# Mixture-of-experts layer on one core: gate-up weights in rows of 32 KB, in places of 4 MB, and an add-back around half of the next gate-up

## The reference

```python
h = h + merged @ w_out[layer]
u = rms_norm(h, ffn_norm_gain[layer])
logits = u @ w_router + b_router
top_logit, top_idx = lax.top_k(logits, 4)          # of 32 experts
top_w = jax.nn.softmax(top_logit, axis=-1)
for e in range(32):                                # only the rows that chose e
    gu = xb @ w_gate_up[e] + b_gate_up[e]          # w_gate_up[e]: 1024 x 2048
    gate, up = jnp.split(gu, 2, axis=-1)
    gate, up = jnp.minimum(gate, 7.0), jnp.clip(up, -7.0, 7.0)
    act = (up + 1.0) * gate * jax.nn.sigmoid(1.702 * gate)
    y_rows = act @ w_down[e] + b_down[e]           # w_down[e]: 1024 x 1024
    h[rows] += y_rows * weight_of_e[rows]
```

## Time and profile before

| | us |
|---|---|
| median of 3 runs | 1256.24 |
| lowest and highest of them | 1252.46, 1256.24 |
| the profiled execution | 1254.52 |
| its span (first to last instruction) | 1252.7 |

### The profile page before, as it was taken

The page is one execution under the profiler, slowest core; times in us unless marked ns, Lnnn a source line. Parts: engine busy times, 40 slices in busy tenths (PEclk is TensorE's granted clock), DMA queues, the critical chain, the costliest instruction groups (busy, mean ns, idle before and its releaser), DMA issues.

```text
span 1252.7 us, 14150 instructions
## 1 busy us (share of the span) xinstructions
PE 1174.1 (94%) x5825; PEld 654.8 (52%) x5825; DVE 302.8 (24%) x551; ACT 133.3 (11%) x270; POOL 6.6 (1%) x14
## 2 busy tenths in 40 slices
PE   9999999999999999999898979898898889898998
PEld 7877888888633435434252534343443434353533
DVE  2154222311302321304030303122121303030322
ACT  2233311101200000101000000001010100000001
POOL 0000001000000000000000000000000000000000
PEclk9999999999999999999999999999999999999999
DMA  9722322336799999999999999999999999999996
GB/s 380 321 97 98 120 102 101 135 134 268 274 417 405 421 427 429 427 427 428 429 428 428 427 430 428 429 428 427 430 429 429 428 427 428 430 430 428 426 421 281
DMA packets 38002, 446.37 MB, mean 356 GB/s; under 512 B 4016, under 2 KB 5168, under 8 KB 6352
## 3 DMA queue, kind: packets, MB, share of 16 engines
q1 hardware_dynamic: 37344, 443.63, 84.8%
q10 hardware_dynamic: 624, 2.25, 0.5%
HBM read 444.81 MB, written 1.05 MB: 356 GB/s over the span
## 4 chain that ended last, share of the span: by engine, by line
PE 68%; DMA 28%; issue 1%; DVE 1%; SPq 0%; ACT 0%; DVEq 0%
DMA ring<-in_w_down 25%; PE ps L513 20%; PE ps L809 18%; PE ps L832 10%; PE ps L772 4%; PE ps L798 3%; DMA ring<-in_w_gate_up 3%; PE ps L863 2%; PE ps L881 2%; PE ps L818 1%; DVE arena L1440 1%; PE ps L853 1%; PE ps L827 0%; PE ps L572 0%; SPq L440 0%
## 5 line engine op out<-in xcount | busy, mean ns | idle before, releaser
L809 PE MATMUL ps<-ring,arena 128*64 128x512 f32 x1392 | 419.5, 613 | 38.7 <-DMA ring<-in_w_gate_up 30.7
L809 PEld LDWEIGHTS ps<-ring,arena 128*64 128x64 f32 x1392 | 137.0, 141 | 303.4 <-issue 303.4
L513 PE MATMUL ps<-arena,ring 128*128 128x256 f32 (+1 forms) x1184 | 268.1, 383 | 1.1 <-DVE arena L1321 1.1
L513 PEld LDWEIGHTS ps<-arena,ring 128*128 128x128 f32 x1184 | 221.0, 189 | 38.9 <-issue 6.6
L832 PE MATMUL ps<-ring,arena 128*64 128x512 f32 x672 | 197.9, 594 | 28.6 <-DMA arena<-in_w_down 18.5
L809 PE MATMUL ps<-arena 128*64 128x512 f32 x464 | 207.1, 599 | 0.0
L832 PEld LDWEIGHTS ps<-ring,arena 128*64 128x64 f32 x672 | 65.4, 137 | 144.9 <-issue 144.9
L1420 DVE COPY arena<-ps 128x1024 f32<-128x1024 f32 x16 | 19.6, 1225 | 421.9 <-PE ps L809 419.0
L832 PE MATMUL ps<-arena 128*64 128x512 f32 x224 | 99.0, 594 | 0.0
L1141 ACT ACTIVATE arena<-ps 128x1024 f32<-128x1024 f32 x16 | 16.4, 1024 | 560.3 <-PE ps L809 555.3
L1413 DVE TENSOR_TENSOR arena<-ps,arena 128x512 f32<-128x512 f32 x64 | 41.1, 684 | 143.2 <-PE ps L818 143.2
(11 more groups left out here) (210 smaller groups left out, 576.4 us busy)
## 6 DMA issues: line engine op xcount, KB each, us to landing
ring<-in_w_gate_up SPq DMA_DIRECT2D x95, 2048.0 KB, 26.9
ring<-in_w_down SPq DMA_DIRECT2D x47, 2048.0 KB, 24.7
arena<-in_w_gate_up SPq DMA_DIRECT2D x32, 2048.0 KB, 31.2
ring<-in_mix_w SPq DMA_DIRECT2D x37, 1024.0 KB, 5.5
arena<-in_w_down SPq DMA_DIRECT2D x16, 2048.0 KB, 26.1
ring<-in_w_down SPq DMA_DIRECT2D x2, 1024.0 KB, 30.6
arena<-in_consts ACTq DMA_DIRECT2D x1, 1424.0 KB, 12.0
arena<-in_xT SPq DMA_DIRECT2D x2, 544.0 KB, 4.4
```

The source lines that it names most:

```text
L513: last = mm(ps[:, PROJ + half, 0:rhs.shape[-1]], w[:, k, half * P:(half + 1) * P], rhs, start=(k == 0), stop=(k == KC - 1))
L809: last = mm(ps[half, bank + b], columns[:, j, half], w[x][:, at:at + 512], start=(j == 0), stop=(j == 7))
```

## The change

1. From pair 2 on (the third pair that the steady loop of loads serves) the gate-up weights come as four "quads" of 4 MB, each with four row blocks of one expert, 32 KB in each partition. There are four places of 4 MB: three quarters of the ring, and one stretch of `arena` (`last_quad`) that joins the two spare ones. Down units stay at 2 MB with 16 KB rows, two of them to a place.
2. SP waits for a place by halves of a gate-up or of a down step. PE's gate-up goes by halves too: `gate_up_quad(m, odd, h)` waits for two quads and does four row blocks.
3. `add_back` of pair m is split: groups 0 and 1 where it was, groups 2 and 3 behind the first half of the next pair's gate-up. The down bias is added in pair 2 instead of pair 1.
4. To let the stretches join, the constants are laid out in another order (the decay tables first, loaded by a third DMA of ACT), `r_u` and `con` move, and the row blocks of the hidden dimension are numbered by four instead of two, in all gate-up sources and in ACT's layout of the tokens (`u2tok`).
5. Ring slots shift by one (`slot_of`), the first gate-up units go to the doubles 0 to 5 and are issued one unit sooner, and the first unit of the second gate-up goes ahead of unit 7.
6. PE writes out pairs 2 and 3 as well; its loop starts at 4.

```diff
-    for name, n in (("ones", P), ("ident", P), ...
-                    ("tri", P), ("from_1", TOK), ("alibi", SCW), ("decay", RH * TOK), ("decay_meta", RH * TOK)):
+    for name, n in (("decay", RH * TOK), ("decay_meta", RH * TOK), ("ones", P), ("ident", P), ...
+                    ("tri", P), ("from_1", TOK), ("alibi", SCW)):
...
+        last_quad = arena[:, end_p - 2048:end_p + 6144]
+        spare = (last_quad[:, 0:4096], arena[:, end_rg - 4096:end_rg], last_quad[:, 4096:8192])
...
+        def slot_of(unit):
+            return (unit + SLOTS - 1) % SLOTS
+        homes = tuple((double(d), pair_landed[d]) for d in range(DOUBLES)) + ((spare[0], spare_landed[0]), (spare[2], spare_landed[2]))
+        def quad(m, n):
+            odd = m if isinstance(m, int) else 0
+            q = ((1 if odd % 2 else 3) + n) % 4
+            return last_quad if q == 3 else ring[:, 4 * q:4 * q + 4].rearrange("p a b -> p (a b)"), quad_landed[q]
+        def half_quad(odd, n):
+            return quad(odd, n // 2)[0][:, 4096 * (n % 2):4096 * (n % 2 + 1)]
...
+            def four_rows_source(lap, n):
+                h, x = divmod(n, 2)
+                return w_gate_up[bass.ds(2 * lap + x, 1), :, :].rearrange("o (h p j) n -> (o p) h (j n)", h=2, j=4)[:, h]
...
             def first_units():
                 for j in (0, 1, 2, 3, 7, 4, 5):
-                    if j < 3:
-                        sp.wait_ge(proj_done, 2 * (27 + 2 * j + 1))
-                    elif j in (3, 7):
+                    if j == 7:
                         sp.wait_ge(proj_read, AT[("wr", KC - 1)] + 1)
+                        dst, arrived, _ = place(0, 0)
+                        sp.dma_start(dst.rearrange("p (o n) -> p o n", o=2), both_experts_source(1, 0)).then_inc(arrived, 16)
                     else:
-                        sp.wait_ge(proj_done, 2 * (33 + 2 * (j - 4) + 1))
+                        sp.wait_ge(proj_done, 2 * (26 + 2 * j + 1))
...
+            def gate_up_quads(m, odd, lap):
                 for n in range(4):
+                    if n < 2:
+                        sp.wait_ge(gu_used, 8 * m + 6 + 2 * n)
+                    else:
+                        sp.wait_ge(dn_used, 4 * m - 6 + 2 * n)
+                    dst, arrived = quad(odd, n)
+                    sp.dma_start(dst, four_rows_source(lap, n)).then_inc(arrived, 16)
+            def down_halves(m, odd, lap):
+                for n in range(4):
+                    sp.wait_ge(gu_used, 8 * m + 10 + 2 * (n // 2))
+                    sp.dma_start(half_quad(odd, 8 + n), down_source(lap, n)).then_inc(down_landed[n], 16)
...
-                pair_units(m, 0, lap_1, lap_0)
-                pair_units(m + 1, 1, lap_2, lap_1)
-            last_gate_up_units(last_m)
-            last_down_units(last_m, 0, 14, 8, 1)
-            last_down_units(last_m + 1, 1, 15, 0, 2)
+                gate_up_quads(m, 0, lap_1)
+                down_halves(m, 0, lap_0)
+                gate_up_quads(m + 1, 1, lap_2)
+                down_halves(m + 1, 1, lap_1)
+            gate_up_quads(last_m, 0, 15)
+            last_down_units(last_m)
...
+            def gate_up_quad(m, odd, h):
+                w = []
+                for x in range(2):
+                    dst, arrived = quad(odd, 2 * h + x)
+                    pe.wait_ge(arrived, 16 * m - 16)
+                    w.append(dst)
+                for jj in range(4):
+                    j = 4 * h + jj
+                    for b in range(4):
+                        at = jj * 2048 + b * 512
+                        for x, half in enumerate(halves):
+                            last = mm(ps[half, GATE + b], xeT[:, j, half], w[x][:, at:at + 512], start=(j == 0), stop=(j == 7))
+                            if jj == 3 and b == 3:
+                                last.then_inc(gu_used, 2)
...
-                    for i in range(4):
-                        gate_up(i, lambda q: place(m, q, odd), xeT)
+                    for h in range(2):
+                        if h == 1 and odd is not None:
+                            add_back(m - 1, (2, 3))
+                        if odd is None:
+                            for i in (2 * h, 2 * h + 1):
+                                gate_up(i, lambda q: place(m, q), xeT)
+                        else:
+                            gate_up_quad(m, odd, h)
...
-                add_back(m, isinstance(m, int) and m == 1)
+                add_back(m, range(4) if isinstance(m, int) and m == 0 else (0, 1))
...
-            with pe.Fori(2, last_m, 2) as m:
+            pair(2, 0)
+            pair(3, 1)
+            with pe.Fori(4, last_m, 2) as m:
...
-                A(u2tok[:, t].rearrange("p (i j f) -> p i j f", i=4, j=2),
-                  ps[:, Y + 2 * t:Y + 2 * t + 2].rearrange("p b f -> p (b f)").rearrange("p (i f j) -> p i j f", i=4, j=2), ACT.Copy,
+                A(u2tok[:, t].rearrange("p (i j f) -> p i j f", i=2, j=4),
+                  ps[:, Y + 2 * t:Y + 2 * t + 2].rearrange("p b f -> p (b f)").rearrange("p (i f j) -> p i j f", i=2, j=4), ACT.Copy,
```

More of the change, by code:

```diff
@@ L79, in _const_layout @@
     at = 0
[L80 to L81 removed]
+    for name, n in (("decay", RH * TOK), ("decay_meta", RH * TOK), ("ones", P), ("ident", P), ("heads2", P), ("halves", 2), ("eps", 1), ("eps64", 1), ("slopes", 2 * HEADS), ("fold", EXPERTS),
+                    ("tri", P), ("from_1", TOK), ("alibi", SCW)):
         CONST_COLS[name] = (at, n)
@@ L87 @@
 N_CONST = _const_layout()
-N_CONST_EARLY = CONST_COLS["tri"][0]
+EARLY, LATE = CONST_COLS["ones"][0], CONST_COLS["tri"][0]
 PARAM_COLS = {}
@@ L221, in build @@
         tmp, sq = (cut(r_tmp, 1024 * i, (2, 2 * TOK)) for i in range(2))
+        r_u = region(KC * ALL)
+        u_sb, u2T = cut(r_u, 0, (KC, ALL)), cut(r_u, 0, (KC, TOK))
+        con = region(N_CONST)
         r_mix = region(ALL)
@@ L413, in second_units @@
             def second_units():
-                for q in range(12):
-                    if q == 0:
-                        sp.wait_ge(proj_done, 2 * NU)
-                    elif q == 1:
+                for q in range(1, 12):
+                    if q == 1:
                         sp.wait_ge(logit_folded, 1)
@@ L500, in project @@
                     pe.wait_ge(proj_read, c)
[L501 removed]
+                w = ring[:, slot_of(unit)].rearrange("p (k n) -> p k n", k=KC)
                 for k in range(KC):
@@ L868, in down_both, with add_back @@
                     last.then_inc(dn_used, 1)
-            def add_back(m, with_bias=False):
+            def add_back(m, groups):
+                with_bias = isinstance(m, int) and m == 2
                 if with_bias:
                     pe.wait_ge(bdown_in, 16)
-                for b in range(4):
+                pe.wait_ge(selwT_ready, m + 1)
+                pe.wait_ge(eout_ready, 2 * m + 2)
+                for b in groups:
                     if not (isinstance(m, int) and 4 * m + b < 2):
@@ L941, in pair @@
                 else:
-                    down(0, [landed_unit(place(m, 8 + x, odd)) for x in range(2)])
+                    down(0, [landed_unit(place(m, 8 + x)) if odd is None else landed_half(m, odd, x) for x in range(2)])
                     turn_hidden(m + 1)
-                    down(1, [landed_unit(place(m, 10 + x, odd)) for x in range(2)])
+                    down(1, [landed_unit(place(m, 10 + x)) if odd is None else landed_half(m, odd, 2 + x) for x in range(2)])
                 turn_weighted(m)
-                if not last_pair:
-                    pe.wait_ge(sel_ready, m + 3)
-                    pe.wait_ge(gate_read, m + 2)
-                    gather(GATE)
-                pe.wait_ge(selwT_ready, m + 1)
-                pe.wait_ge(eout_ready, 2 * m + 2)
-                add_back(m, isinstance(m, int) and m == 1)
+                pe.wait_ge(sel_ready, m + 3)
+                pe.wait_ge(gate_read, m + 2)
+                gather(GATE)
+                add_back(m, range(4) if isinstance(m, int) and m == 0 else (0, 1))
             pe.wait_ge(u2tok_ready, 2)
```

93 lines of the change are left out of this document (43 added, 50 removed).

## The result

The changed kernel takes 1268.09 us (median of 4 runs, 1264.12 to 1270.82) against 1255.39 for the kernel before: **slower by 1.1%, ratio 1.0112, interval 1.0095 to 1.0129**, or 14.1 us (11.9 to 16.2), where the two medians are 12.7 us apart. The range given was 1252.5 to 1264.5, with 1258.3 as the value. The profiled execution took 1264.12 us, with a span of 1262.3 against 1252.7.

The account below looks back on a forecast made before the run. The stream of weight loads was taken to set the steady pace, with PE's work after the last gate-up landing setting the end: 1254.5 - 3.7 + 6.85 = 1257.7, or 1259.4 with a slow last half; predicted 1258.3, range 1252.5 to 1264.5.

Parts of the forecast that it names:

- Part 1: Gate-up loads: 32 KB rows as one packet save 0.071 us a quad, 3.7 us over 52 quads.
- Part 2: End of the kernel: 13.94 us of gate-up remain after the last quad lands instead of 7.09, adding 6.85 us.
- Part 3: Steady stream: 4 MB places come free after a half, still early enough; costs nothing while slacks of 2.1 to 3.7 us hold.
- these slacks: Time left when places come free, after 2.0 us from issue to flow: 3.7 and 3.6 us steady, 2.1 at the tightest.
- one hole: Thin stretch after SP's issue at 393.95 us, about 2 us, 221 GB/s; 2.0 us from issue to flow was taken.
- 3.6 + 2.0: Down loads' place: half 0 done at 33.3, wanted at 38.9; 3.6 us slack plus 2.0 from issue to flow.
- Part 6: Half-rate clock after PE's waits: hidden by the stream, except 1.7 us if the last half is slowed, even chances.
- Now the stream hides it: Claim that about 1.7 us of PE time lost to a half-rate stretch costs nothing in the steady part.
- the stream breaks: Rival: coarser places come back too late; 1284 if 1 us late, some 1267 if part of a us; chance 0.09.
- a slowed half with a slow engine behind it: One way named for the rival of a broken stream to use up the slacks of 2.1 to 3.7 us.
- Parts 4 and 5: Split add-back and bias move, then the start (slots, load order, constants, token layout, written-out pairs): no effect on time.

Follow-up runs that it names:

- f_mid5: The changed kernel with five added matmuls (2.5 us) in the middle of every gate-up half, none in the waits: 1284.62 us, ratio 1.0237.
- a_early: The changed kernel with the first two down loads of a pair waiting for a quarter of the gate-up instead of a half: 1261.24 us, ratio 1.0046.
- a_fill: The changed kernel with unread matmuls in PE's waits, five ahead of each second gate-up half, four ahead of first halves from pair 3: 1256.50 us, ratio 1.0032.
- f_unsplit: The changed kernel with add-back in one piece and eight unread matmuls ahead of each second half, none ahead of the first: 1257.39 us, ratio 1.0022.
- c_best: a_fill without added matmuls in the last pair and with all of the last gate-up in eight loads of 2 MB: 1250.57 us, ratio 0.9978.
- b_written_out: The kernel before with pairs 2 to 7 written out in PE's program ahead of the loop: 1256.68 us, ratio 1.0019.
- c_best2: c_best with down loads waiting for a quarter of the gate-up and PE's loop from pair 2 again: 1250.60 us, ratio 0.9975.

## Why the prediction was wrong

- **Part 1, the rows: right.** One packet for a row of 32 KB, 58.44 us a pair in an unbroken stream against 58.74, 3.8 us in 13 pairs.
- **Part 2, a half in place of a quarter at the end: right in size.** 9.66 us more behind the last landing, of which 6.85 as forecast; with the last gate-up in quarters, 5.9 us were won back.
- **Part 3, "Cost nothing, as long as these slacks hold": this is the step that failed.** It took 2.0 us from an issue to its data flowing, read from one hole in which few data moved (221 GB/s). In a full stream that is too short a lead: by `f_mid5` places given back 3.0 us ahead cost 1.8 us a pair, and in the changed kernel and `a_early` leads of 3.5 to 3.9 us cost between 0 and 1.4 us. The other half of the slack was right: a half at the full clock is done 5.5 us before its place is wanted, where the prediction had 3.6 + 2.0, and that is enough (`a_fill`). With a slow half (3.8) it isn't always. That the 16 DMA engines are out of step, as at the end, would explain why one lead does for some pairs and not for others; it is not shown.
- **Part 6, the clock: right about the size, 1.7 us a slow half, and wrong in "Now the stream hides it".** I priced it for the last half alone. A slow half also gives its place back later, and with the lead of part 3 mis-sized it broke the stream: 8.5 us in twelve pairs. In the last half it was dearer than 1.7: two slow stretches in a row, 2.9 us.
- **The rival "the stream breaks" was the one that came true**, priced at "some 1267" with a chance of 0.09. Its condition, "a slowed half with a slow engine behind it", was written down and then not worked out against the 2.1 to 3.7 us of slack.
- **Parts 4 and 5: as said.** The split add-back does nothing (`f_unsplit`); the written-out pairs cost about 1 us at most, not quite nothing. Nothing at the start comes from the change, but the start itself differs by 2 us from profile to profile (the gather at 333 us), which part 5 did not reckon with.

In sum, by the ratios: -3.8 for the rows and +6.9 for the half at the end give +3.1, where `a_fill` measured +4.0 (1.8 to 6.1). The late places and the slow last half, which `a_fill` takes away, are the other 10 of the +14.1 us measured.

**Still open.** Why a lead of 3.5 to 3.9 us is enough in one pair and 1.4 us short in another; nor was it looked into which of the 16 engines lags. In `a_fill` and `c_best` the pairs before about 711 us lose 1.5 to 2.3 us in all, though places come back 5.5 us ahead. All of these losses fall into stretches in which one or two instruction packets were fetched: `a_fill` has seven from 500 to 700 us, one more up to 711, and none from there to 1200, where its pairs take 58.43 to 58.48 us. The kernel before has one in its last, longer pair, `a_fill` none there. Yet in `b_written_out` some packets cost 1.0 us and some nothing, and `c_best2`, with fewer of them and its pairs at 58.4 us up to the last, has no better median. That a packet is to blame is therefore a guess.

## What to carry to other kernels

When the loads set the pace, what keeps their stream whole is how early places come back. Larger places come back later, in steps as long as PE's work on them. Work out that lead for the slowest PE (a clock at half rate after a wait), and against a lead measured in a running stream, not at a standstill. Where an engine has time to spare but its lateness is passed on, matmuls that nobody reads can pay: here they saved some 10 us. At the very end cut the loads small again: what counts there is the work behind the last landing.

## What was unexpected in the hardware

- A DMA issued 3.5 us before the one ahead of it lands can be too late to keep the loads flowing (262 GB/s from 730 to 732 us), and can be early enough (issue at 964.23). With 5.5 us no pair of `a_fill` behind 711 us was longer than 58.48.
- The start differs by 2 us between profiles of kernels that are the same up to there: 32 small matmuls at 333 us take 5.44 us at half rate or 3.81 us, and the whole stream of weights follows (issues at 393.95 or 391.89 us).
- Small differences in a wait went with the granted clock. In the rows of the changed kernel above, the second halves behind waits of 1.83 to 1.86 us (732.57, 967.87, 1026.29) took 13.95 us, and the one behind 2.20 us (792.38) took 15.65, one stretch at half rate. With 2 to 2.5 us of matmuls put into each wait (`a_fill`), the granted clock stayed at 1.00 from 400 to 1200 us.
- Twelve more instruction packets of 16 KB in a full stream cost 2.4 us (1.1 to 3.6).
